# Wide products for expert_u up to tile 62, one piece of memory for both halves of the tokens, and another split of the subtraction between DVE and POOL

## The chip, the cores and the metric

The kernel runs on one core of a Trainium2 chip. The metric is the device time of one execution in microseconds. The engines are PE (TensorE, matrix products), DVE (VectorE), ACT (ScalarE), POOL (GpSimd) and SP (SyncE, which issues most of the DMAs). Each works through its own list of instructions in order, and they meet by semaphores only.

## The reference, cut to what matters

Two transformer blocks follow each other on 256 tokens of width 1024, in float32. The change is in the last part of the second block, a layer with 16384 small experts. Each is one row of `expert_u` and one row of `expert_v`.

```
q = rmsnorm(x) @ w_query                       # 8 heads, two halves of 128
s = scores of each half against 128 sub_keys   # per head: 128 + 128 scores
i1, i2, gates = top 16 of the 16 x 16 best pairs, softmax over them
a = gelu(rmsnorm(x) @ expert_u.T)              # 256 tokens x 16384 experts
out = x + sum over the 8 * 16 chosen (gate * a) * expert_v row
```

The kernel computes the activations of all 16384 experts densely, multiplies them by a map of gates that is zero nearly everywhere, and multiplies the result by `expert_v`. That is done so for 192 of the 256 tokens; the other 64 fetch their rows of `expert_v` by indirect DMAs.

## The kernel before

**Halves.** PE multiplies in a format of less than full precision (`fp32r`). So each operand is split in a high part (a copy in that format, made by ACT, `act_high`) and a low part (the rest, a subtraction). Three of the four products of parts are computed: high by high, high by low, low by high. The subtraction is in place on the tile, and its 2048 columns are divided: DVE (`dve_low`) takes the first `share_of(...)`, POOL (`pool_low`) the others, and PE waits for both (`lo_v`, `lo_g`). The share is `EVEN` = 1152 for the first `ROOMY` = 45 tiles of `expert_u`, 1536 for the others of it, and 2048 for `expert_v`.

**Tiles.** `expert_u` comes in 64 tiles of 1 MB (128 x 2048), each with two groups of 128 experts and eight chunks of the width. The first 45 go through a ring of five places in SBUF, the others through a ring of three, since the gate maps and activations (`W`) grow over the other places. A tile of the ring is loaded when the tile that had its place has been used by PE.

**Wide and narrow products.** In tiles 0 to 46 (`WIDE` = 47) the high part of a chunk is multiplied by both halves of the tokens at once, 512 columns (L1277, for the last chunk L1280), which land beside each other in PSUM, and its low part by the high half, 256 columns (L1278). The low sums are then copied out of PSUM by ACT (L2797, into `LP`) and added to the high ones by DVE (`add_halves`, L2141, both in PSUM and LP). After that ACT applies GELU (L2802, L2810). From tile 47 on three products of 256 columns each add up in PSUM themselves (`pe_pass3`, L546 to L548), and ACT applies GELU directly.

**Gate maps.** In tiles 47 to 62 each tile also has three maps (`early_quads`), each of four tokens: one-hot rows by ACT (two pieces, L2757 and L2761), DVE (L2108, L2110) and POOL (L2881), which PE multiplies (L1260) into banks 0 to 3. DVE then weighs the activations with them (L2120, L2121, L2128).

**Routing.** In tiles 1 to 46 DVE also finds the chosen experts, a piece for each tile (`ROUTING`, `dve_route`), for tokens 0 to 127 in tiles 1 to 23 and for the others in 24 to 46. Eight tiles of "lists" (MAX8 and the like), one of "pairs" (eight sums L2235), five of "heads" (MAX8 again), one of "gates", six of "select" (comparison L2270, eight products L2274, reduction L2276, and the same again), one of "share". After tiles 22 and 45 PE transposes what "share" left.

**Order of DVE in an iteration i.** `add_halves(i-1)`, then `dve_low` of tile i+1, then the routing piece (from tile 47 on: one-hots, weighing, `dve_low`). ACT: high part of tile i+2, then for tile i the copy of the low sums, waiting for DVE's sum, GELU. POOL: subtractions alone until tile 47. PE takes tile n when both subtractions are done and GELU of tile n-2.

Of the kernel before, what the change touches and what calls it, by code (L numbers as in the profile page):

```python
# [27 lines left out]
LAST_MAPS = MAPS_AT + DENSE // 4 // MAPS  # L28
WIDE = 47
ROOMY = 45  # L30
EVEN = 1152
MOE_PLACES = (0, 1, 2, 3, 4, 5, 6, 9, 10, 11, 12, 13, 14, 15)
# [167 lines left out]
def buffers(nc):  # L200
# [26 lines left out]
    m.HT = (fr(m.HH[:, :, :]), fr(m.HL[:, :, :]))  # L227
    m.HX = fr(halves[:, :, :, :]).rearrange("p x k t -> p k x t")
    m.Y = twin("y", [P, 2, D])
# [107 lines left out]
    m.SC = DS[:, 4096:8192].rearrange("p (b j n) -> p b j n", b=2, j=16)  # L337
    m.LP = [BIG[:, 19456 + 512 * i:19968 + 512 * i].rearrange("p (n t) -> p n t", n=2) for i in range(2)]
    m.W = BIG[:, 0:128 * DENSE].rearrange("p (n t) -> p n t", n=128)
# [33 lines left out]
def weight_tiles(a, m):  # L373
# [74 lines left out]
    last_in = lambda x: max([k for k in range(len(slot)) if slot[k] == x] + high_in.get(x, []))  # L448
    order = sorted((0, 1, 2, 5, 6), key=last_in)
    slot += [order[i % 5] for i in range(ROOMY)]  # L450
# [659 lines left out]
def tensor_second(nc, m, s, t, before, after):  # L1110
# [153 lines left out]
    for i in range(64):  # L1264
        tile = f["expert_u"] + i
        hi, lo = pe_halves(pe, m, s, t, tile)
        bank = act_bank(i)
        if i < 2:
            pe.wait_ge(s.sc, 6 + 2 * i)
        else:  # L1270
            pe.wait_ge(s.act, i - 1)
        for j in range(2 if i < WIDE else 0):
            o = m.PS[:, bank + j, :].rearrange("p (x t) -> p x t", x=2)
            for k in range(8):
                at = 1024 * j + 128 * k
                if k < 7:
                    pe.matmul(o, hi[:, at:at + P], m.HX[:, k], start=(k == 0), stop=False, skip_group_check=True)  # L1277
                ins = pe.matmul(o[:, 0], lo[:, at:at + P], m.HT[0][:, k, :], start=False, stop=False, skip_group_check=True)  # L1278
                if k == 7:
                    ins = pe.matmul(o, hi[:, at:at + P], m.HX[:, k], start=False, stop=True, skip_group_check=True)  # L1280
        for j in range(2 if i >= WIDE else 0):
            for k in range(8):
                at = 1024 * j + 128 * k
                ins = pe_pass3(pe, m.PS[:, bank, 256 * j:256 * j + 256], [x[:, at:at + P] for x in (hi, lo)],
                               [x[:, k, :] for x in m.HT], k == 0, k == 7)
        ins.then_inc(s.used, 2)
        for what, b, _ in ROUTING.get(i, ()):
# [58 lines left out]
def act_bank(i):  # L1346

    return 4 + 2 * (i % 2) if i < WIDE else 6 + i % 2


def act_columns(m, i):

    x, bank = m.PS, act_bank(i)
    return x[:, bank:bank + 2, 0:256] if i < WIDE else x[:, bank, :].rearrange("p (n t) -> p n t", n=2)


# [536 lines left out]
def vector_second(nc, m, s, t, before, after, own):  # L1893
# [62 lines left out]
    def beat(i, beats=BEATS2):  # L1956
        for what, u in beats.get(i, ()):
# [3 lines left out]
            elif what == "peerturn":  # L1961
                dve_turn(nc, m, s, "peer", m.g_ffn2, m.HT[1], m.HT[0])
            elif what == "outaturn":
# [174 lines left out]
    def add_halves(i):  # L2138
        bank = act_bank(i)
        ve.wait_ge(s.part, 1 + i + 1)  # L2140
        ve.tensor_tensor(m.PS[:, bank:bank + 2, 0:256], m.PS[:, bank:bank + 2, 0:256], m.LP[i % 2], ALU.add).then_inc(s.added, 1)  # L2141

# [463 lines left out]
def scalar_second(nc, a, m, s, t, before, after, own):  # L2606
# [35 lines left out]
    def beat(i, beats=BEATS2):  # L2642
        for what, u in beats.get(i, ()):
# [35 lines left out]
            elif what == "outaturn":  # L2679
                act_turn(nc, m, s, "outa", m.gkp[:, 8:16], m.HT[0])  # L2680
                act_group(nc, m, s, o, "outa", m.ossb, 1)
            elif what == "ME":
                if u == 12:
                    act_know(nc, s, "cross")
                act_mem_exps(u)
            elif what == "MC":
                act_mem_copy(u)
            elif what == "peernorm":
                act_know(nc, s, "ffn2")
                for b in range(2):  # L2690
                    ins = ac.activation(m.Y[:, b, :], m.X[:, b, :], ACT.Copy, scale=rs[:, b:b + 1])
                ins.then_inc(s.peer_n, 1)
            elif what == "peerturn":
                act_turn(nc, m, s, "peer", m.g_ffn2, m.HT[0])

# [79 lines left out]
    for i in range(64):  # L2775
        if i < ROOMY:
            act_high(nc, m, s, t, first + i + 2)
        elif i > ROOMY:
            act_high(nc, m, s, t, first + i + 1)
# [16 lines left out]
        if i < WIDE:  # L2796
            ac.activation(m.LP[i % 2], m.PS[:, act_bank(i):act_bank(i) + 2, 256:512], ACT.Copy).then_inc(s.part, 1)  # L2797
            ac.wait_ge(s.added, i + 1)
# [421 lines left out]
```

## Time and profile before

| | |
|---|---|
| median of 3 runs | 1590.06 us (1589.67 to 1591.22) |
| profiled execution | 1590.42 us |
| its span, first to last instruction | 1589.1 us |
| PE busy | 1528.3 us (96%) |
| DVE, ACT, POOL busy | 957.0, 715.4, 536.6 us |
| granted clock of PE, mean | 0.997 |

The span is what the trace shows of the execution. A busy share is a mean over stages with different limits. What an engine waits for stands in brackets in the timeline and in the view of waits; an engine that is not waited for may be idle without cost.

### The profile page before, as it was taken

What the parts mean: (1) busy time and instruction counts of PE and PEld (TensorE: products, weight loads), DVE (VectorE), ACT (ScalarE), POOL (GpSimd) and SP (SyncE); (2) the same over time, 40 slices, a digit from 0 to 9 for tenths busy, and PEclk for the clock granted to TensorE, in tenths of its full rate; (3) what the DMA queues carried; (4) which work ended last, traced back from release to release, by engine and by line L of the source; (5) the groups of instructions that cost most, each with busy time, mean ns of one, the idle gap of its engine ahead of it and who ended that gap; (6) DMA issues with size and microseconds to landing.
All of it is one profiled execution on the core that took longest, in us unless ns stands there. A gap on an engine that the chain in (4) does not pass through costs nothing.

```text
span 1589.1 us, 22128 instructions
## 1 busy us (share of the span) xinstructions
PE 1528.3 (96%) x8741; PEld 1170.4 (74%) x8741; DVE 957.0 (60%) x1658; ACT 715.4 (45%) x1091; POOL 536.6 (34%) x322
## 2 busy tenths in 40 slices
PE   8999999999889888999999999999999999999998
PEld 6789754445344333888989888888899988888886
DVE  5876522111111111767553699899777869999896
ACT  6666411101001100656452656556588855555544
POOL 4212000000000000413121434434487866888880
PEclk9999999999999999999999999999999999999999
DMA  8457999999999999744443666666443479999994
GB/s 314 145 185 266 399 374 420 421 422 421 422 421 421 421 421 415 255 144 165 141 158 118 237 197 197 200 198 197 144 141 120 163 285 327 359 363 361 359 377 154
DMA packets 100749, 446.85 MB, mean 281 GB/s; under 512 B 11536, under 2 KB 20240, under 8 KB 59040
## 3 DMA queue, kind: packets, MB, share of 16 engines
q1 hardware_dynamic: 86976, 405.96, 68.0%
q0 software_dynamic: 11264, 33.60, 5.7%
q10 hardware_dynamic: 2400, 5.81, 0.9%
q8 instruction: 72, 1.18, 0.3%
q14 instruction: 37, 0.30, 0.1%
HBM read 436.31 MB, written 8.91 MB: 280 GB/s over the span
## 4 chain that ended last, share of the span: by engine, by line
PE 76%; DMA 16%; DVE 4%; ACT 2%; issue 1%; SPq 0%; ACTq 0%; DVEq 0%
PE ps L785 12%; PE ps L1324 10%; PE ps L1277 10%; DMA fix<-in_w_up 7%; PE ps L1316 7%; PE ps L546 7%; PE ps L548 6%; PE ps L547 6%; PE ps L1278 6%; DMA big<-in_w_up 5%; PE ps L1260 3%; DMA halves<-in_w_up 2%; PE ps L1280 1%; PE ps L807 1%; PE ps L852 1%
## 5 line engine op out<-in xcount | busy, mean ns | idle before, releaser
L2853 POOL TENSOR_TENSOR big_parts<-big,fix_parts 128x896 fp32r<-128x896 f32 (+1 forms) x23 | 47.3, 2056 | 551.7 <-ACT fix_parts L2327 551.7
L785 PE MATMUL ps<-big 128*64 128x512 f32 x792 | 212.7, 594 | 19.2 <-DMA big<-in_w_up 8.4
L2327 ACT ACTIVATE fix_parts<-fix 128x2048 fp32r<-128x2048 f32 x71 | 136.0, 1919 | 75.9 <-PE ps L1324 46.2
L785 PEld LDWEIGHTS ps<-big 128*64 128x64 f32 x792 | 71.0, 137 | 131.9 <-issue 130.3
L1277 PE MATMUL ps<-halves_parts,fix_parts 128*128 128x512 f32 x434 | 155.8, 398 | 0.0
L1378 DVE TENSOR_TENSOR fix_parts<-fix,fix_parts 128x1536 fp32r<-128x1536 f32 (+2 forms) x72 | 140.0, 1946 | 23.1 <-ACT fix_parts L2327 19.8
L785 PE MATMUL ps<-fix,big 128*64 128x512 f32 x488 | 133.4, 594 | 9.4 <-DMA fix<-in_w_up 6.6
L2853 POOL TENSOR_TENSOR fix_parts<-fix,fix_parts 128x512 fp32r<-128x512 f32 (+1 forms) x47 | 89.0, 1895 | 155.7 <-ACT fix_parts L2327 145.3
L1856 DVE TENSOR_TENSOR big<-big,ps 128x512 f32<-128x512 f32 x16 | 11.0, 688 | 215.3 <-PE ps L785 215.3
L1278 PE MATMUL ps<-halves_parts,fix_parts 128*128 128x256 f32 x464 | 120.7, 281 | 0.0
L548 PE MATMUL ps<-halves_parts,fix_parts 128*128 128x256 f32 x416 | 117.6, 283 | 0.0
L2905 POOL DMA_INDIRECT small<-actkeep,tig x64 | 109.2, 1706 | 19.5 <-issue 19.5
L2327 ACT ACTIVATE fix_parts<-big 128x2048 fp32r<-128x2048 f32 x41 | 78.5, 1915 | 41.0 <-PE ps L1324 28.5
L1879 DVE SCALAR_TENSOR_TENSOR big_parts<-ps,small,big_parts 128x512 fp32r<-128x512 f32 x32 | 22.6, 747 | 119.8 <-ACT big_parts L2599 119.8
L1277 PEld LDWEIGHTS ps<-halves_parts,fix_parts 128*128 128x128 f32 x434 | 81.7, 188 | 17.1 <-issue 0.2
L2874 POOL DMA_INDIRECT big<-in_expert_v,tig x48 | 81.7, 1702 | 34.5 <-issue 13.1
L1278 PEld LDWEIGHTS ps<-halves_parts,fix_parts 128*128 128x128 f32 x464 | 87.6, 189 | 5.3
L785 PEld LDWEIGHTS ps<-fix,big 128*64 128x64 f32 x488 | 45.2, 137 | 60.9 <-issue 60.9
L2599 ACT ACTIVATE big_parts<-ps,small 128x512 fp32r<-128x512 f32 x32 | 20.2, 683 | 145.7 <-PE ps L785 145.7
L1378 DVE TENSOR_TENSOR big_parts<-big,fix_parts 128x2048 fp32r<-128x2048 f32 (+2 forms) x41 | 80.2, 1957 | 8.6 <-ACT fix_parts L2327 6.6
L2563 ACT ACTIVATE big<-ps,small 128x256 f32<-128x256 f32 x32 | 13.4, 470 | 151.3 <-PE ps L807 151.3
L1277 PE MATMUL ps<-halves_parts,x_parts 128*128 128x512 f32 x224 | 80.4, 398 | 1.1 <-ACT big L2745 1.1
(450 smaller groups left out, 4205.5 us busy)
## 6 DMA issues: line engine op xcount, KB each, us to landing
fix<-in_expert_u SPq DMA_DIRECT2D x46, 1024.0 KB
fix<-in_expert_v SPq DMA_DIRECT2D x38, 1024.0 KB
big<-in_w_down SPq DMA_DIRECT2D x36, 1024.0 KB, 26.0
big<-in_w_up SPq DMA_DIRECT2D x32, 1024.0 KB, 26.4
big<-in_w_gate SPq DMA_DIRECT2D x31, 1024.0 KB, 23.3
big<-in_expert_v SPq DMA_DIRECT2D x26, 1024.0 KB
fix<-in_w_up SPq DMA_DIRECT2D x23, 1024.0 KB, 26.4
fix<-in_w_gate SPq DMA_DIRECT2D x21, 1024.0 KB, 26.6
```

The lines of the kernel that those rows point to most:

```text
L546: pe.matmul(o, l[0], r[0], start=first, stop=False)
L547: pe.matmul(o, l[0], r[1], start=False, stop=False)
L548: return pe.matmul(o, l[1], r[0], start=False, stop=last)
L785: ins = pe.matmul(m.PS[64 * i:64 * i + 64, bank, :], lhs(h * k_of // 2 + k, i), view(t.place[t.slot[x]])[:, k, c0:c0 + 512], start=(h + k ...
L1277: pe.matmul(o, hi[:, at:at + P], m.HX[:, k], start=(k == 0), stop=False, skip_group_check=True)
L1278: ins = pe.matmul(o[:, 0], lo[:, at:at + P], m.HT[0][:, k, :], start=False, stop=False, skip_group_check=True)
L1316: ins = pe.matmul(m.PS[:, 2 + half, :], both[:, j, 0:P], v[y][:, 1024 * j + 512 * half:1024 * j + 512 * half + 512], start=(i + j + y == 0 ...
L1324: ins = pe.matmul(m.PS[:, half, :], both[:, j, P + P * x:2 * P + P * x], v[y][:, 1024 * j + 512 * half:1024 * j + 512 * half + 512], start ...
L1378: nc.vector.tensor_tensor(m.fr(x[:, 0:end]), x[:, 0:end], m.fr(hi[:, 0:end]).bitcast(F32), ALU.subtract).then_inc(s.lo_v, 1)
L2327: nc.scalar.activation(m.fr(t.high[n]), t.place[slot], ACT.Copy).then_inc(s.hi, 1)
L2853: nc.gpsimd.tensor_tensor(m.fr(x[:, at:2048]), x[:, at:2048], m.fr(hi[:, at:2048]).bitcast(F32), ALU.subtract).then_inc(s.lo_g, 1)
L2905: po.indirect_dma_start(m.pk[:, k:k + 1], None, acts, bass.IndirectOffsetOnAxis(m.aix[:, k:k + 1], 0)).then_inc(s.picked[k // 4 % 4], 16)
```

## The change

Six things change. Tiles 47 to 62 get the wide products too (`WIDE` = 63), beside the gate maps, with the copy of the low sums in another place (`low_part`). Five places serve tiles 0 to 46 (`ROOMY` = 47), and the high part of tile 47 is made an iteration earlier. DVE subtracts 512 columns instead of 1152 in these tiles, and POOL the other 1536 (`EVEN`). Tiles 0 and 1 write banks 0 to 3, and tiles 0 to 3 wait for fewer of the eight copies of the scores. The two halves of the tokens lie chunk by chunk beside each other, so that the 512 columns are one piece of memory and not two of 256.

```diff
-WIDE = 47
-ROOMY = 45
-EVEN = 1152
+WIDE = 63
+ROOMY = 47
+EVEN = 512
...
-    m.HX = fr(halves[:, :, :, :]).rearrange("p x k t -> p k x t")
+    m.HX = fr(halves[:, :, :, :].rearrange("p x k t -> p (x k t)")).rearrange("p (k x t) -> p k x t", k=8, x=2)
+    m.HTX = (m.HX[:, :, 0], m.HX[:, :, 1])
...
-    order = sorted((0, 1, 2, 5, 6), key=last_in)
+    order = sorted(range(3), key=last_in) + [5, 6]
...
-        if i < 2:
-            pe.wait_ge(s.sc, 6 + 2 * i)
+        if i < 4:
+            pe.wait_ge(s.sc, 2 + 2 * i)
...
-                ins = pe.matmul(o[:, 0], lo[:, at:at + P], m.HT[0][:, k, :], start=False, stop=False, skip_group_check=True)
+                ins = pe.matmul(o[:, 0], lo[:, at:at + P], m.HTX[0][:, k, :], start=False, stop=False, skip_group_check=True)
...
-    return 4 + 2 * (i % 2) if i < WIDE else 6 + i % 2
+    return 2 * i if i < 2 else 4 + 2 * (i % 2) if i < WIDE else 6 + i % 2
...
+def low_part(m, i):
+
+    return m.LP[i % 2 + (2 if i >= MAPS_AT else 0)]
...
-        if i < ROOMY:
+        if i < MAPS_AT - 1:
             act_high(nc, m, s, t, first + i + 2)
-        elif i > ROOMY:
+        elif i >= MAPS_AT:
             act_high(nc, m, s, t, first + i + 1)
...
-            ac.activation(m.LP[i % 2], m.PS[:, act_bank(i):act_bank(i) + 2, 256:512], ACT.Copy).then_inc(s.part, 1)
+            ac.activation(low_part(m, i), m.PS[:, act_bank(i):act_bank(i) + 2, 256:512], ACT.Copy).then_inc(s.part, 1)
```

DVE in two tiles of "select", before. L2141 is the sum of the parts, L1378 the subtraction (`fix` and `big` are places of the ring, `x_parts` and `fix_parts` high parts), L2274 and L2276 routing.

```order
L2141 TENSOR_TENSOR ps<-ps,big 128x2x256
L1378 TENSOR_TENSOR big_parts_51<-big,x_parts_54 128x1152
L2274 TENSOR_TENSOR big<-big,y 128x256 x8
L2141 TENSOR_TENSOR ps<-ps,big 128x2x256
L1378 TENSOR_TENSOR big_parts_51<-big,fix_parts_53 128x1152
L2276 TENSOR_REDUCE y<-big 128x128
```

The same tiles of the change (lines are six further down), and nothing has moved but the size of the subtraction:

```order
L2147 TENSOR_TENSOR ps<-ps,big 128x2x256
L1384 TENSOR_TENSOR big_parts_51<-big,x_parts_54 128x512
L2280 TENSOR_TENSOR big<-big,y 128x256 x8
L2147 TENSOR_TENSOR ps<-ps,big 128x2x256
L1384 TENSOR_TENSOR big_parts_51<-big,fix_parts_53 128x512
L2282 TENSOR_REDUCE y<-big 128x128
```

POOL at the first four tiles of `expert_u`, where only its size changes likewise, before:

```order
L2853 TENSOR_TENSOR fix_parts_53<-fix,x_parts_54 128x896
L2853 TENSOR_TENSOR fix_parts_53<-fix,fix_parts_53 128x896 x2
L2853 TENSOR_TENSOR big_parts_51<-big,x_parts_54 128x896
```

and in the change, each with 640 columns more:

```order
L2859 TENSOR_TENSOR fix_parts_53<-fix,x_parts_54 128x1536
L2859 TENSOR_TENSOR fix_parts_53<-fix,fix_parts_53 128x1536 x2
L2859 TENSOR_TENSOR big_parts_51<-big,x_parts_54 128x1536
```

ACT from the high part of tile 46 to GELU of tile 47, before (L2327 makes a high part, L2797 copies low sums, L2757 and L2761 are one-hots, L2802 to L2810 GELU):

```order
L2797 ACTIVATE big<-ps 128x512
L2802 ACTIVATE y<-ps 128x128
L2810 ACTIVATE big<-ps 128x384
L2797 ACTIVATE big<-ps 128x512
L2802 ACTIVATE y<-ps 128x128
L2810 ACTIVATE big<-ps 128x384
L2327 ACTIVATE fix_parts_53<-fix 128x2048
L2797 ACTIVATE big<-ps 128x512
L2802 ACTIVATE y<-ps 128x128
L2810 ACTIVATE big<-ps 128x384
L2327 ACTIVATE x_parts_54<-fix 128x2048
```

and in the change: the high part of tile 47 stands ahead of the copy of tile 45 and no longer behind its GELU.

```order
L2803 ACTIVATE big<-ps 128x512
L2808 ACTIVATE y<-ps 128x128
L2816 ACTIVATE big<-ps 128x384
L2333 ACTIVATE fix_parts_53<-fix 128x2048
L2803 ACTIVATE big<-ps 128x512
L2808 ACTIVATE y<-ps 128x128
L2816 ACTIVATE big<-ps 128x384
L2803 ACTIVATE big<-ps 128x512
L2808 ACTIVATE y<-ps 128x128
L2816 ACTIVATE big<-ps 128x384
L2333 ACTIVATE x_parts_54<-fix 128x2048
```

In tile 47 and after, ACT also gets the copy of the low sums (L2803) between the one-hots and GELU:

```order
L2763 ACTIVATE y<-ii,tig 128x128 x2
L2767 ACTIVATE y<-y,tig 128x128 x2
L2803 ACTIVATE big<-ps 128x512
L2808 ACTIVATE y<-ps 128x128
L2813 ACTIVATE big<-ps 128x24
L2816 ACTIVATE big<-ps 128x2x180
```

DVE gets the sum L2147 ahead of its one-hots there.

## Rows read from the trace of the kernel before

**Rows 1.** The page: busy time of each engine, share of the span, instructions.

```profile
PE 1528.3 (96%) x8741; PEld 1170.4 (74%) x8741; DVE 957.0 (60%) x1658; ACT 715.4 (45%) x1091; POOL 536.6 (34%) x322
```

**Rows 2.** Windows: busy us of PE, PEld, DVE, ACT, POOL; clock, DMA share, GB/s.

```profile
880.37:1146.30 265.93, 265.92 (x1510) 230.91 (x1510) 232.47 (x568) 150.05 (x193) 104.21 (x47) 1.00 0.58 190
1146.30:1282.40 136.10, 135.12 (x1153) 135.07 (x1153) 108.60 (x201) 113.44 (x259) 110.39 (x89) 1.00 0.44 141
```

**Rows 3.** Waits of PE from 880 to 1300: total us, times, longest.

```profile
PE ps L1277 <- ACT big L2745: 1.1, 1, 1.1
PE ps L546 <- issue: 1.0, 1, 1.0
```

**Rows 4.** Timeline of ACT, tiles 41 and 42: start, us, instruction, idle before and releaser.

```profile
1117.87 0.60 ACT L2797 ACTIVATE big<-ps 128x512 f32<-128x512 f32 x1 [0.63 <-PE ps L1280]
1119.24 0.28 ACT L2802 ACTIVATE y<-ps 128x128 f32<-128x128 f32 x1 [0.77 <-DVE ps L2141]
...
1119.78 1.92 ACT L2327 ACTIVATE fix_parts<-big 128x2048 fp32r<-128x2048 f32 x1
1123.51 0.60 ACT L2797 ACTIVATE big<-ps 128x512 f32<-128x512 f32 x1 [1.81 <-PE ps L1280]
```

**Rows 5.** Timelines of DVE, POOL and ACT around tile 17.

```profile
979.40 4.69 DVE L2274 TENSOR_TENSOR big<-big,y 128x256 f32<-128x256 f32 x8
984.01 0.68 DVE L2141 TENSOR_TENSOR ps<-ps,big 128x512 f32<-128x512 f32 x1
...
980.99 2.15 POOL L2853 TENSOR_TENSOR big_parts<-big,fix_parts 128x896 fp32r<-128x896 f32 x1 [2.73 <-ACT fix_parts L2327]
...
982.18 0.60 ACT L2797 ACTIVATE big<-ps 128x512 f32<-128x512 f32 x1 [1.27 <-PE ps L1280]
984.73 0.28 ACT L2802 ACTIVATE y<-ps 128x128 f32<-128x128 f32 x1 [1.95 <-DVE ps L2141]
```

**Rows 6.** Timeline of POOL: one subtraction of 896 columns, one of 512.

```profile
987.27 2.12 POOL L2853 TENSOR_TENSOR fix_parts<-fix,fix_parts 128x896 fp32r<-128x896 f32 x1 [4.14 <-ACT fix_parts L2327]
...
1242.82 1.29 POOL L2853 TENSOR_TENSOR fix_parts<-fix,fix_parts 128x512 fp32r<-128x512 f32 x1
```

**Rows 7.** Groups of DVE from 880 to 1147: busy us, mean ns of one, idle before.

```profile
L2270 DVE TENSOR_TENSOR big<-ii,y 128x2048 f32<-128x2048 f32 x4 | 9.1, 2279 | 0.0
...
L2276 DVE TENSOR_REDUCE y<-big 128x128 f32<-128x2048 f32 x4 | 9.1, 2272 | 0.0
...
L1378 DVE TENSOR_TENSOR fix_parts<-fix,fix_parts 128x1536 fp32r<-128x1536 f32 x2 | 3.5, 1752 | 2.5 <-ACT fix_parts L2327 2.5
```

**Rows 8.** Timelines of DVE and POOL ahead of tile 0, and PE's first product.

```profile
876.97 1.36 DVE L1378 TENSOR_TENSOR fix_parts<-fix,x_parts 128x1152 fp32r<-128x1152 f32 x1 [4.05 <-ACT x_parts L2327]
...
877.01 3.25 POOL L2853 TENSOR_TENSOR fix_parts<-fix,x_parts 128x896 fp32r<-128x896 f32 x1 [25.26 <-ACT x_parts L2327]
...
880.36 0.47 PE L1277 MATMUL ps<-halves_parts,x_parts 128*128 128x512 f32 x1 [1.09 <-ACT big L2745]
```

**Rows 9.** Timelines of PE and POOL: tile 46, and tile 48 with its maps.

```profile
1140.48 0.47 PE L1277 MATMUL ps<-halves_parts,fix_parts 128*128 128x512 f32 x1
...
1145.90 0.40 PE L1280 MATMUL ps<-halves_parts,fix_parts 128*128 128x512 f32 x1
...
1155.84 0.36 PE L546 MATMUL ps<-halves_parts,x_parts 128*128 128x256 f32 x1
...
1161.68 1.95 PE L1260 MATMUL ps<-big 128*128 128x128 f32 x16
...
1164.28 0.36 PE L546 MATMUL ps<-halves_parts,fix_parts 128*128 128x256 f32 x1
...
1144.34 2.84 POOL L2853 TENSOR_TENSOR fix_parts<-fix,fix_parts 128x512 fp32r<-128x512 f32 x1 [9.86 <-ACT fix_parts L2327]
```

**Rows 10.** Timeline of ACT behind tile 58: GELU, and the last one-hots.

```profile
1246.21 0.28 ACT L2802 ACTIVATE y<-ps 128x128 f32<-128x128 f32 x1 [1.42 <-PE ps L548]
...
1252.34 0.88 ACT L2761 ACTIVATE y<-y,tig 128x128 f32<-128x128 f32 x2
```

More of the change, by code:

```diff
@@ L337, in buffers @@
     m.SC = DS[:, 4096:8192].rearrange("p (b j n) -> p b j n", b=2, j=16)
-    m.LP = [BIG[:, 19456 + 512 * i:19968 + 512 * i].rearrange("p (n t) -> p n t", n=2) for i in range(2)]
+    m.LP = [x.rearrange("p (n t) -> p n t", n=2) for x in (BIG[:, 19456:19968], BIG[:, 19968:20480], DS[:, 0:512], DS[:, 512:1024])]
     m.W = BIG[:, 0:128 * DENSE].rearrange("p (n t) -> p n t", n=128)
@@ L1284, in tensor_second @@
                 ins = pe_pass3(pe, m.PS[:, bank, 256 * j:256 * j + 256], [x[:, at:at + P] for x in (hi, lo)],
-                               [x[:, k, :] for x in m.HT], k == 0, k == 7)
+                               [x[:, k, :] for x in m.HTX], k == 0, k == 7)
         ins.then_inc(s.used, 2)
@@ L1961, in beat @@
             elif what == "peerturn":
-                dve_turn(nc, m, s, "peer", m.g_ffn2, m.HT[1], m.HT[0])
+                dve_turn(nc, m, s, "peer", m.g_ffn2, m.HTX[1], m.HTX[0])
             elif what == "outaturn":
@@ L2140, in add_halves @@
         ve.wait_ge(s.part, 1 + i + 1)
-        ve.tensor_tensor(m.PS[:, bank:bank + 2, 0:256], m.PS[:, bank:bank + 2, 0:256], m.LP[i % 2], ALU.add).then_inc(s.added, 1)
+        ve.tensor_tensor(m.PS[:, bank:bank + 2, 0:256], m.PS[:, bank:bank + 2, 0:256], low_part(m, i), ALU.add).then_inc(s.added, 1)
     dve_low(nc, m, s, t, first)
@@ L2693, in beat @@
             elif what == "peerturn":
-                act_turn(nc, m, s, "peer", m.g_ffn2, m.HT[0])
+                act_turn(nc, m, s, "peer", m.g_ffn2, m.HTX[0])
     def product(tile, at=None, beats=BEATS2):
```

## The prediction

> **What bounds the kernel now.** I read the page first: PE is busy for 1528.3 of 1589.1 us, DVE for 957.0 [rows 1]. The windows then divide what the change touches: tiles 0 to 46 of expert_u (880.37 to 1146.30, 47 tiles) and tiles 47 to 62 with the gate maps (to 1282.40). PE is busy for 265.92 of 265.93 us in the first and 135.12 of 136.10 in the second [rows 2]. The view of waits has only two for PE in this stretch: 1.1 us ahead of tile 0 and 1.0 us ahead of tile 47 [rows 3]. So a faster DVE, ACT or POOL gives back at most 2 us here, and a slower one costs as soon as its slack is used up. Hence the question is how much slack there is, and that is read in the timeline.
>
> In a wide tile PE needs 5.64 us (1117.87 to 1123.51, the copies that start 0.03 us behind a tile's end). A tile's results go: copy of the low sums by ACT, sum by DVE, GELU by ACT 1.37 us after the copy began, and at 1.91 us the next high part, 1.85 us long [rows 4]. That releases DVE's and POOL's subtractions for a later tile. PE takes tile n+2 only when GELU of tile n is done: so DVE's sum may begin up to about 5.64 - 0.60 - 0.04 - 0.60 = 4.4 us behind a tile's end, where it begins about 0.67 us behind it in a plain tile. In some it is later already: tile 17's copy begins at 982.18, its sum at 984.01, and GELU waited 1.95 us for DVE [rows 5] against 0.77 us in a plain tile [rows 4].
>
> **What each part costs.** (a) *EVEN 512*. DVE subtracts 512 columns instead of 1152, POOL 1536 instead of 896, in tiles 0 to 44; in 45 and 46 POOL takes 1536 instead of 512. POOL takes 1.29 us for 512 columns and 2.12 for 896 [rows 6], so 2.12 + 640 x 0.83/384 = 3.50 us for 1536. DVE takes 1.36 us for 1152 when it comes first [rows 8] and 1.75 for 1536 [rows 7], so 0.67 for 512.
>
> By mere busy time that fits: POOL 3.5 of 5.64 us, and DVE gains 0.67 us a tile. But the two hold each other up. In tile 17 DVE runs eight equal products L2274. They take 4.69 us, and POOL's 2.15 us from 980.99 lies on them [rows 5]. Without a hold they follow each other at 0.335 us (each 256 columns at the 2.28 us that 2048 take [rows 7], and a little over), 2.68 us in all: the hold is 2.0 us, POOL's whole operation. It goes both ways: at 877.01 POOL started 0.04 us behind DVE's 1.36 us and took 3.25 instead of 2.12 us [rows 8]. The reduction L2276 reads one operand only; its four average 2272 ns, and POOL's 2.12 us at 987.27 lies on one of them unstretched [rows 6, 7]. So subtractions, L2235, L2270 and L2274, with two operands in SBUF, wait for POOL to finish and POOL for them; MAX8, reductions and sums on PSUM don't.
>
> The Trainium skill states this rule ("SBUF — State Buffer", section "SBUF: two separate sides"): DVE with two SBUF inputs and GpSimd exclude each other for a whole instruction. The trace agrees. By busy time alone this part would add 0 to the sum, by the rule what is worked out next.
>
> What DVE needs in an iteration that holds one whole POOL operation: sum 0.60, own subtraction 0.60, the routing piece, and 3.5 of hold. The routing pieces of "select" are 2.20 (L2270), 2.68 (eight L2274), 2.20 (L2276) [rows 7, 5]. That is 6.9, 7.4 and 6.9 us against a period of 5.64. Now it is 0.60 + 1.28 + 2.68 + 2.1 = 6.7 in the worst, and one tile of a reduction without a hold (4.1) repairs it. With the change no select tile is under 5.64, and six follow each other: (6.9 + 7.4 + 6.9 - 3 x 5.64) x 2 = 8.6 us late, for each of the two routing blocks. The tiles ahead of them, "pairs" and "heads", are late as well.
>
> I carried this forward tile by tile on paper, with these durations and three rules: whoever asks first runs its whole operation alone; POOL asks 3.3 us after DVE's sum began; PE starts tile n+2 after GELU of tile n. As a test, the kernel before comes out with the sum of tile 17 at 1.5 us behind the tile's end, where the trace has 1.87 [rows 5] (the end is 982.14), and without a stall, as in the trace [rows 3]. With the change, the sum of tile 9 comes at 2.7 us, 10 2.9, 11 0.9, 12 3.4, 13 1.4, 14 3.9, 15 2.0, 16 5.3, 17 6.9, 18 4.1, 19 5.8, 20 7.1, 21 4.1. From 16 on this is past 4.4: PE waits ahead of tiles 18 to 22 for 0.8, 1.6, 0.3, 1.1 and 1.6 us, and after tile 22, where its transposes need DVE's "share", for 3.8. In the second block (tiles 39 to 45) the same, with about 1.1 at the share: 9.3 + 6.6 = 15.9 us. Moving a queueing overhead by 0.02 us per operation, POOL's time by 0.1 us, or the hold that overlaps by 0.13 us gives 9 to 19 us. I take **+16**.
>
> (b) *The start.* Banks 0 to 3 for tiles 0 and 1 let PE start when two score banks are copied, not six. But POOL's first subtraction ended at 880.26, just before PE's start at 880.36 [rows 8]. It becomes 0.6 of hold + 3.5 - 0.15 = 3.97 us instead of 3.25: **+0.7**. Tile 1's, released by the same kind of copy, grows alike.
>
> (c) *Tile 47.* Its high part moves from iteration 46 to 45, so POOL's subtraction, which ran until 1147.18 [rows 9] while PE waited [rows 3], is long done: the 1.0 us wait goes. What is late next is ACT: from the end of tile 46 it needs 1.37 + 0.54 + 1.81 + 4.5 (twelve one-hot halves) = 8.2 us until the third map can run, so the maps of 47 end 9.1 us behind it instead of 9.5: **-0.4**.
>
> (d) *Wide tiles with maps.* Now a tile takes 8.44 us: 5.84 of products (1155.84 to 1161.68) and 2.60 of maps. Wide, right behind a pause of the same kind, it was 1140.48 to 1145.90 + 0.24 = 5.66 [rows 9]: PE's period becomes 8.26. ACT adds copy and wait, 1.37 us, to 6.91 of GELU, high part and one-hots (1246.21 to 1252.34 + 0.78) [rows 10]: 8.28. The two are even; before, ACT had 1.42 us to spare. DVE, busy for 108.60 us in these 16 tiles [rows 2], 6.8 each, gets 0.6 more and stays under it. 15 x (8.44 - 8.28) = **-2.4**. From both sides: nothing if ACT's chain is 0.16 longer, +2 if it is 0.3 longer.
>
> (e) *Layout of the halves.* The 512 columns become one piece of memory. A pair of products takes 5.64/16 = 0.3525 us in the steady stage, 0.347 right after a pause, both with the two pieces [rows 4, 9]. Two pieces thus cost nothing in one of the modes. I take 0; the other bound is 0.0055 x 16 x 47 = -4.1.
>
> The sum: 16 + 0.7 - 0.4 - 2.4 = +13.9 us. The profiled execution took 1590.42 us with a span of 1589.1, 0.4 above the median of 1590.06; on the median the forecast is 1604.0.
>
> **Rivals.** *No stalls* (ends on the other side): the sums stay under 4.4 us, because a DVE operation slips in more often between POOL's, or POOL's 1536 columns take under about 2.9 us. With 768 columns for DVE and 2.95 us for POOL my paper gives 4 to 10 us, so this is the point where it is decided. Then 0.7 - 0.4 - 2.4 = -2.1: 1588.0. For it: 0 stalls now. Against: a hold of a whole operation, seen in L2274 and in POOL's first subtraction. *No stalls and a faster layout*: -6.2, 1583.9. *Stalls, and the layout gains*: 1604.0 less 2 to 4, about 1601; a stalled tile gives back nothing. *Stalls of a smaller size*: one block's share wait vanishes, about 8 us in all: 1596. *The maps' stage slows*: DVE's longer iterations catch ACT's copy, +0.3 a tile: 1604.0 + 7 = 1611.
>
> **Chances.** Stalls as worked out 0.47, with the layout's gain 0.15, smaller stalls 0.13, slower maps as well 0.08, no stalls 0.12, no stalls and a faster layout 0.05. A measurement of this kernel tells 0.2% (3.2 us) from no change. Slower is the first four, 0.82 (0.01 of smaller stalls to "same"); same 0.12; faster 0.06. The range 1595 to 1611 takes in the first four and leaves out the last two; these bounds are also those of the stalls, 7 and 20 us, with the other terms.
>
> **What the profile after would show.** DVE subtractions of 512 columns and POOL's of 1536 at about 3.5 us; eight L2274 (some lines further down) taking 6.2 us; DVE's sums up to 7 us behind a tile's end; PE waits of 7 to 10 us ahead of tiles 18 to 23 and of 5 to 8 us ahead of tiles 41 to 46, put down to DVE or ACT; tile 0 at about +0.7; the wait ahead of tile 47 gone; 8.3 us from maps to maps. If PE shows no wait between tiles 16 and 23, step (a) is wrong; if the pair of products takes 0.347 us in a plain tile, (e) is.

## The result, and the profile after

| | before | after |
|---|---|---|
| median of 4 runs | 1590.36 us (1589.67 to 1591.22) | 1600.28 us (1599.96 to 1601.94) |
| ratio, 95% interval | | 1.0067 (1.0054 to 1.0079) |
| span of the profiled execution | 1589.1 us | 1598.7 us |
| granted clock of PE, mean | 0.997 | 0.995 |

The kernel became 9.9 us slower. The page of the kernel after, busy time of each engine (before: [rows 1]):

```profile
PE 1528.9 (96%) x8485; PEld 1158.1 (72%) x8485; DVE 976.7 (61%) x1674; ACT 722.2 (45%) x1107; POOL 587.9 (37%) x322
```

PE does as much as before. Where it stands still is in the windows of the kernel after: tiles 0 to 46, tiles 47 to 62 with the maps, and the rest (columns as in [rows 2], with the bounds set at the same places):

```profile
881.72:1159.68 277.96, 269.39 (x1511) 232.33 (x1512) 246.68 (x570) 148.13 (x192) 172.32 (x52) 0.99 0.55 181
1159.68:1292.94 133.26, 132.58 (x897) 120.99 (x896) 113.19 (x210) 118.83 (x272) 91.72 (x84) 1.00 0.43 143
1292.94:1598.65 305.71, 298.46 (x1338) 246.18 (x1336) 268.36 (x292) 157.19 (x147) 218.40 (x128) 0.99 0.89 332
```

Against [rows 2] tiles 0 to 46 are 277.96 - 265.93 = 12.03 us longer and the maps' stage 136.10 - 133.26 = 2.84 us shorter. Ahead of them lie 1.35 us more (881.71 against 880.36). What follows the maps is 1.0 us shorter (305.71 against 1589.1 - 1282.4 = 306.7). Sum: 12.03 - 2.84 + 1.35 - 1.0 = 9.5, the 9.6 of the spans.

PE's waits in the kernel after, from 870 to 1310 (before, [rows 3], there were two of about 1 us):

```profile
PE ps L1294 <- DVE y L2290: 4.7, 2, 3.4
PE ps L1278 <- ACT big L2816: 2.6, 4, 1.0
PE ps L1278 <- issue: 2.0, 1, 2.0
PE ps L1278 <- DVE fix_parts L1384: 0.6, 1, 0.6
PE ps L1278 <- DVE big_parts L1384: 0.5, 1, 0.5
PE ps L1261 <- ACT big L2767: 0.3, 1, 0.3
PE ps L1261 <- ACT y L2767: 0.3, 1, 0.3
```

The first line is the wait for "share" (3.4 us after tile 22, 1.3 after tile 45). The "ACT big" waits are those for GELU, which itself waits for DVE's late sum; "issue" is the start of tile 0, and the last two are waits for one-hots ahead of the second and third map of tile 47. Read by tile, PE stands ahead of 18, 19, 22 and 41, 42, 45 for 1.0, 0.55, 0.3 and 1.0, 0.55, 0.3 us. With the shares that is 8.5 us. POOL's and DVE's subtractions, from 881 to 1150, grouped; for DVE shortest, median and longest in ns:

```profile
L2859 POOL TENSOR_TENSOR fix_parts<-fix,fix_parts 128x1536 fp32r<-128x1536 f32 x19 | 69.4, 3657 | 41.9 <-ACT fix_parts L2333 41.9
...
L1384 DVE TENSOR_TENSOR big_parts<-big,fix_parts x12: 674/1424/3405, 900.2 to 1136.2; 128x512 fp32r<-128x512 f32 x12
```

The same 512 columns take DVE from 0.67 to 3.4 us. The timelines of DVE and of POOL around tiles 17 to 19 show why:

```profile
977.47 5.60 DVE L2276 TENSOR_TENSOR big<-ii,y 128x2048 f32<-128x2048 f32 x1
982.99 0.69 DVE L2147 TENSOR_TENSOR ps<-ps,big 128x512 f32<-128x512 f32 x1
983.59 0.68 DVE L1384 TENSOR_TENSOR big_parts<-big,x_parts 128x512 fp32r<-128x512 f32 x1
984.19 2.76 DVE L2280 TENSOR_TENSOR big<-big,y 128x256 f32<-128x256 f32 x8
986.87 0.69 DVE L2147 TENSOR_TENSOR ps<-ps,big 128x512 f32<-128x512 f32 x1
987.47 3.40 DVE L1384 TENSOR_TENSOR big_parts<-big,fix_parts 128x512 fp32r<-128x512 f32 x1
990.80 2.27 DVE L2282 TENSOR_REDUCE y<-big 128x128 f32<-128x2048 f32 x1
...
973.48 3.51 POOL L2859 TENSOR_TENSOR fix_parts<-fix,fix_parts 128x1536 fp32r<-128x1536 f32 x1 [4.43 <-ACT fix_parts L2333]
977.20 3.71 POOL L2859 TENSOR_TENSOR big_parts<-big,x_parts 128x1536 fp32r<-128x1536 f32 x1 [0.21 <-ACT x_parts L2333]
986.25 4.08 POOL L2859 TENSOR_TENSOR big_parts<-big,fix_parts 128x1536 fp32r<-128x1536 f32 x1 [5.34 <-ACT fix_parts L2333]
990.29 3.97 POOL L2859 TENSOR_TENSOR fix_parts<-fix,fix_parts 128x1536 fp32r<-128x1536 f32 x1
```

The comparison that begins at 977.47 takes 5.60 us instead of 2.28: until POOL ends at 980.91 it does nothing. DVE's subtraction at 987.47 takes 3.40 instead of 0.68, until POOL ends at 990.33. Then POOL's next waits for it (3.97 instead of 3.50), and the reduction at 990.80 runs at full speed beside POOL. That is a hold by whole operations.

### The profile page after: what moved, and what is told of

The parts are those of the page before. It is cut to its first block, busy times and chain, and to the rows that moved or that the text cites. A ratio compares the mean times of both kernels' runs of the same rounds, so it can differ in the third digit from the quotient of the medians.

```text
span 1598.7 us, 21648 instructions
## 1 busy us (share of the span) xinstructions
PE 1528.9 (96%) x8485; PEld 1158.1 (72%) x8485; DVE 976.7 (61%) x1674; ACT 722.2 (45%) x1107; POOL 587.9 (37%) x322
## 4 chain that ended last, share of the span: by engine, by line
PE 63%; DMA 16%; DVE 12%; POOL 4%; ACT 3%; issue 3%; SPq 0%; ACTq 0%; DVEq 0%
PE ps L786 12%; PE ps L1278 8%; PE ps L1325 7%; DMA fix<-in_w_up 7%; DMA big<-in_w_up 5%; PE ps L1317 5%; PE ps L547 5%; PE ps L1279 5%; PE ps L549 5%; PE ps L548 5%; PE ps L1261 3%; DVE fix_parts L1384 2%; POOL small L2911 2%; DMA halves<-in_w_up 2%; POOL big L2880 1%
## 5 line engine op out<-in xcount | busy, mean ns | idle before, releaser
L2859 POOL TENSOR_TENSOR big_parts<-big,fix_parts 128x1536 fp32r<-128x1536 f32 (+1 forms) x23 | 64.6, 2811 | 543.2 <-ACT fix_parts L2333 543.2
L1278 PE MATMUL ps<-halves_parts,fix_parts 128*128 128x512 f32 x588 | 212.6, 400 | 1.9 <-ACT big L2816 1.4
L1279 PE MATMUL ps<-halves_parts,fix_parts 128*128 128x256 f32 x720 | 187.0, 280 | 0.0
L2333 ACT ACTIVATE fix_parts<-fix 128x2048 fp32r<-128x2048 f32 x71 | 136.1, 1920 | 73.1 <-PE ps L1325 48.5
L2859 POOL TENSOR_TENSOR fix_parts<-fix,fix_parts 128x512 fp32r<-128x512 f32 (+1 forms) x47 | 113.7, 2420 | 126.9 <-ACT fix_parts L2333 116.7
L786 PE MATMUL ps<-fix,big 128*64 128x512 f32 x488 | 133.6, 594 | 9.2 <-DMA fix<-in_w_up 6.6
L1279 PEld LDWEIGHTS ps<-halves_parts,fix_parts 128*128 128x128 f32 x720 | 135.8, 189 | 7.1
L1278 PEld LDWEIGHTS ps<-halves_parts,fix_parts 128*128 128x128 f32 x588 | 111.1, 189 | 26.1 <-DVE fix_parts L1384 2.3
L1278 PE MATMUL ps<-halves_parts,x_parts 128*128 128x512 f32 x294 | 105.9, 399 | 4.0 <-issue 2.0
L1384 DVE TENSOR_TENSOR big_parts<-big,fix_parts 128x2048 fp32r<-128x2048 f32 (+2 forms) x41 | 85.2, 2080 | 9.5 <-ACT fix_parts L2333 8.7
L1325 PE MATMUL ps<-fix_parts,y_parts 128*128 128x512 f32 x268 | 78.4, 389 | 0.0
```

Source lines behind the costliest of these rows:

```text
L786: ins = pe.matmul(m.PS[64 * i:64 * i + 64, bank, :], lhs(h * k_of // 2 + k, i), view(t.place[t.slot[x]])[:, k, c0:c0 + 512], start=(h + k ...
L1279: ins = pe.matmul(o[:, 0], lo[:, at:at + P], m.HTX[0][:, k, :], start=False, stop=False, skip_group_check=True)
L1325: ins = pe.matmul(m.PS[:, half, :], both[:, j, P + P * x:2 * P + P * x], v[y][:, 1024 * j + 512 * half:1024 * j + 512 * half + 512], start ...
L1384: nc.vector.tensor_tensor(m.fr(x[:, 0:end]), x[:, 0:end], m.fr(hi[:, 0:end]).bitcast(F32), ALU.subtract).then_inc(s.lo_v, 1)
L2333: nc.scalar.activation(m.fr(t.high[n]), t.place[slot], ACT.Copy).then_inc(s.hi, 1)
L2859: nc.gpsimd.tensor_tensor(m.fr(x[:, at:2048]), x[:, at:2048], m.fr(hi[:, at:2048]).bitcast(F32), ALU.subtract).then_inc(s.lo_g, 1)
```

## The experiments

All are against the kernel before, run on the same chip. The stages in this table are worked out from each profiled execution: from the first product of tile 0 to the last of tile 46, to the end of the last map, to the end of the span. Their bounds differ from those of the windows above by up to 0.3 us.

| kernel | tiles 0-46 | 47-62 | rest | median us | ratio (95%) |
|---|---|---|---|---|---|
| before | 265.8 | 136.5 | 306.5 | | 1 |
| after | 277.8 | 133.6 | 305.5 | 1600.28 | 1.0067 (1.0054 to 1.0079) |
| e1 after, EVEN 1152 | 265.9 | 133.7 | 305.2 | 1587.77 | 0.9982 (0.9973 to 0.9991) |
| e2 before, EVEN 512 | 276.1 | 136.4 | 305.5 | 1600.87 | 1.0064 (1.0050 to 1.0077) |
| e3 e1, old layout | 265.7 | 133.7 | 306.1 | 1587.17 | 0.9980 (0.9971 to 0.9989) |
| e4 512 in calm tiles only | 265.9 | 133.7 | 305.8 | 1587.77 | 0.9985 (0.9976 to 0.9994) |
| e5 after, EVEN 768 | 272.6 | 133.6 | 305.4 | 1594.75 | 1.0036 (1.0023 to 1.0049) |
| e6 after, EVEN 1024 | 265.8 | 133.6 | 305.3 | 1586.65 | 0.9982 (0.9973 to 0.9991) |
| e7 POOL in two pieces | 273.2 | 133.6 | 305.1 | 1594.11 | 1.0036 (1.0023 to 1.0049) |
| e8 share's transposes later | 277.2 | 133.7 | 305.3 | 1598.73 | 1.0058 (1.0045 to 1.0071) |
| e9 the kernel after again | 278.8 | 133.7 | 306.7 | 1599.28 | 1.0061 (1.0047 to 1.0074) |
| e10 e1, tile 0 mostly on DVE | 266.6 | 133.6 | 305.1 | 1586.61 | 0.9982 (0.9972 to 0.9991) |
| e13 e1, WIDE 47 | 265.8 | 136.2 | 307.8 | 1588.68 | 0.9992 (0.9983 to 1.0001) |
| e14 e1, POOL works longer | 281.1 | 133.7 | 306.4 | 1603.30 | 1.0081 (1.0068 to 1.0095) |

The median of before was 1590.17 beside e1 to e4, 1589.16 beside e5 and e7 to e9, and 1589.87 beside the others; the ratios allow for it. Theory H is the prediction's: POOL's operation holds DVE's. The rest of the span varied from 305.1 to 307.8 with no pattern, so nothing is read from it.

**e1: the split alone undone.**

```diff
-EVEN = 512
+EVEN = 1152
```

> The changed kernel with EVEN back at 1152, all else as changed. Theory H (POOL's subtraction of 1536 columns holds DVE's operations with two operands in SBUF, so DVE's sums come late beside the routing pieces and PE waits): no wait of PE between tiles 16 and 23 or 39 and 46, tiles 0 to 46 in about 266 us as before, 8.25 us per tile with maps; 1590.4 - 2.9 (maps) - 0.4 (tile 47) = about 1587, the ratio to before 0.998. Rival R (the split is not what costs; the banks, the moved high parts, the slots or wide tiles with maps are): stays at about 1600.

Measured: 1587.77, ratio 0.9982. In the waits of PE all but the start and those ahead of the second and third map of tile 47 are gone:

```profile
PE ps L1278 <- issue: 1.0, 1, 1.0
PE ps L1261 <- ACT big L2767: 0.3, 1, 0.3
PE ps L1261 <- ACT y L2767: 0.3, 1, 0.3
```

The whole loss comes of the split, and without it the change would have been a gain of 0.2%.

**e2: the split alone made, in the kernel before.**

```diff
-EVEN = 1152
+EVEN = 512
```

> The kernel before with EVEN 512 and nothing else changed. Theory H: the same waits as in the changed kernel, ahead of tiles 18, 19, 22 and at both shares, about 8.6 us of waits, with the slower clock behind the first share and the start 12 to 13 us in all; 1602 to 1604. Rival R: within 1 us of the kernel before.

Measured: 1600.87, and PE's waits are those of the kernel after at the first share and ahead of 18, 19, 22, 41 and 42:

```profile
PE ps L1293 <- DVE y L2284: 3.4, 1, 3.4
PE ps L1277 <- ACT big L2810: 2.3, 3, 1.0
```

Theory H holds; its size was 1 to 3 us too high. The stage is 10.3 us longer and not 12, for the second share finds nothing to wait for. Here tiles 45 and 46 are still split 1536 to 512, so POOL's last two operations are short; that this is the reason is argued and not tested by itself.

**e3: the old layout under EVEN 1152.**

```diff
-    m.HX = fr(halves[:, :, :, :].rearrange("p x k t -> p (x k t)")).rearrange("p (k x t) -> p k x t", k=8, x=2)
-    m.HTX = (m.HX[:, :, 0], m.HX[:, :, 1])
+    m.HX = fr(halves[:, :, :, :]).rearrange("p x k t -> p x k t")
+    m.HTX = m.HT
```

> The changed kernel with EVEN 1152 and the halves in their old layout (the 512 columns of a product in two pieces again). The prediction's step (e), layout costs nothing: within 0.5 us of the same kernel with the new layout, 5.64 us per plain tile in both. Rival (one piece is faster, hidden in the changed kernel by stalls): 2 to 4 us slower than with the new layout.

Measured: 1587.17 against 1587.77, and 265.7 against 265.9 us for tiles 0 to 46. The layout gives nothing.

**e4: 512 columns where DVE has short pieces, 1152 elsewhere.**

```diff
-    return EVEN if 0 <= i < ROOMY else SHARE if i < 64 else 2048
+    busy = 8 <= i <= 24 or 31 <= i < ROOMY
+    return (1152 if busy else EVEN) if 0 <= i < ROOMY else SHARE if i < 64 else 2048
```

> The changed kernel with 512 columns for DVE only in tiles 0 to 7 and 25 to 30 of expert_u, whose subtractions stand beside the short lists, and 1152 in the tiles whose subtractions stand beside pairs, heads and select. Theory H: no wait of PE in tiles 16 to 46, the start 0.7 us later: about 1588. Rival (1536 columns on POOL cost in every tile, by contention with PE's or ACT's reads): 14 of 47 tiles keep 30% of the 12 us, about 1591.

Measured: 1587.77, stage 265.9, no wait of PE there. POOL's 3.5 us cost nothing in these 14 tiles, beside the lists. So the loss comes from the other 33, and the waits of PE above stand among those with long pieces that have two operands in SBUF.

**e5 and e6: other sizes.** EVEN 768 and 1024 in the kernel after.

> The changed kernel with EVEN 768: POOL subtracts 1280 columns, 2.12 + 384 x 0.83/384 = 2.95 us. Theory H: the same lateness, much smaller; the paper of the prediction gives 3 to 8.5 us of stalls, less what it over-counted with 512 (16 against 12): 1587.8 + 3 = about 1591. Rival T (a threshold that lies above 2.95 us): no wait, 1588. Rival in proportion to the columns moved: 0.6 of the 12.5 us, 1595.

> The changed kernel with EVEN 1024: POOL subtracts 1024 columns, 2.12 + 128 x 0.83/384 = 2.4 us. The rule carried forward on paper gives 0 to 1 us of stalls: 1588. Rival (the loss is in proportion to the columns moved, as 768 with 6.8 of 12 us might suggest): 0.2 x 12.5 = 2.5 us more, 1590.3.

Measured: 1594.75 with 768 and 1586.65 with 1024. The stage grows by 6.8 us with 768 and by nothing with 1024. So the loss is not in proportion to the columns: it begins between 2.39 us of POOL (1024 columns) and 2.95 us (768). With 768, H's number (1591) was too low, though the 6.8 us lie in the 4 to 10 that the prediction's paper gave, and the rival in proportion hit 1595 by chance, as 1024 then showed.

**e7: POOL's columns in two operations.**

```diff
-    nc.gpsimd.tensor_tensor(m.fr(x[:, at:2048]), x[:, at:2048], m.fr(hi[:, at:2048]).bitcast(F32),
-                            ALU.subtract).then_inc(s.lo_g, 1)
+    cuts = (at, (at + 2048) // 2, 2048) if at == EVEN else (at, 2048)
+    for lo, to in zip(cuts, cuts[1:]):
+        ins = nc.gpsimd.tensor_tensor(m.fr(x[:, lo:to]), x[:, lo:to], m.fr(hi[:, lo:to]).bitcast(F32), ALU.subtract)
+    ins.then_inc(s.lo_g, 1)
```

> The changed kernel with EVEN 512, POOL's 1536 columns subtracted in two operations of 768 (about 1.84 us each). Theory H (POOL holds DVE for a whole operation, and DVE can come in between two): DVE's compare is held 1.8 us instead of 3.5, its sum before it is not later; PE's waits fall to less than half: 1590 to 1595, although POOL is busy for 0.2 us longer per tile. Rival (both engines share the path by the amount of data, or POOL keeps it while it has work): 1600 or a little more.

Measured: 1594.11. POOL is busy for longer (191.8 us in tiles 0 to 46 against 172.3), and yet the stage is 4.6 us shorter. The same comparison as above, in the timeline of DVE of this kernel:

```profile
973.88 3.94 DVE L2276 TENSOR_TENSOR big<-ii,y 128x2048 f32<-128x2048 f32 x1
977.92 0.70 DVE L2147 TENSOR_TENSOR ps<-ps,big 128x512 f32<-128x512 f32 x1
978.53 1.54 DVE L1384 TENSOR_TENSOR big_parts<-big,x_parts 128x512 fp32r<-128x512 f32 x1
980.00 7.71 DVE L2280 TENSOR_TENSOR big<-big,y 128x256 f32<-128x256 f32 x8
```

It is held for one piece, 3.94 - 2.28 = 1.7 us instead of 3.3. The eight products, between which both pieces find a gap, take more instead (7.71 us); so six tenths of the loss stay, 7.4 of 12 us, where less than half was the claim for PE's waits. The time is in the range expected, 1590 to 1595.

**e8: the first share's transposes one tile later.** PE makes them behind tile 23.

```diff
-        for what, b, _ in ROUTING.get(i, ()):
+        for what, b, _ in ROUTING.get(i - 1, ()) if i == 23 else ROUTING.get(i, ()) if i != 22 else ():
             if what == "share":
```

> The changed kernel (EVEN 512) with TensorE's three transposes of the first share behind tile 23 instead of tile 22. The wait there was 3.4 us, and tile 23 then ran its first pairs of products at a granted clock of 0.5 (0.63 us a pair instead of 0.35). If both are paid only because PE stands still: the wait and the slow pairs go, 3.4 + 1.3 us, as DVE's sum of tile 22 begins 3.4 us behind the tile, under the 4.4 that are allowed: about 1595.5. Rival (the wait only moves: PE stands ahead of tile 23 or 24 for DVE's sum): 1599 to 1600.

Measured: 1598.73, stage 277.2. The 3.4 us wait went, but PE now waits 2.3 us ahead of tile 25, for ACT behind DVE:

```profile
PE ps L1278 <- ACT big L2816: 4.9, 5, 2.3
```

The rival held: the wait moved, to a tile later than it said, and the median lies 0.3 us under its range. DVE's "keys" and "sparse" pieces stand behind the transposes, so DVE waited with them; its sum of tile 23 then came 6.7 us behind the tile's end. I had looked at the sum of tile 22 and not at what is queued behind the moved wait.

**e9: the kernel after once more.** It was to have POOL's share cut to 896 columns; the edit did not get into the kernel, and what ran was the kernel after, unchanged.

> The changed kernel with EVEN 512, but POOL subtracts only columns 1152 to 2047 (columns 512 to 1151 get no low part subtracted: this part of the computation is left out). Tells the length of POOL's operation from what DVE does. Theory H: POOL holds DVE for 2.1 us, DVE itself works for 0.7 us less: no wait of PE, sums earlier than with EVEN 1152, about 1587.5. Rival (the lateness comes of the order in which DVE gets its work, not of POOL's length): 1600.

Measured: 1599.28, so it tells nothing of that expectation. It does tell how repeatable the lateness is. Its stage is 278.8 us against 277.8. At tile 9 POOL's subtraction starts 3.95 us behind the end of tile 8 in the one and 3.94 in the other, beside DVE's "pairs" sums, but it takes another time. The timeline of POOL in the kernel after, and then in this one:

```profile
936.76 4.67 POOL L2859 TENSOR_TENSOR fix_parts<-fix,fix_parts 128x1536 fp32r<-128x1536 f32 x1 [2.13 <-ACT fix_parts L2333]
```

```profile
934.95 3.64 POOL L2859 TENSOR_TENSOR fix_parts<-fix,fix_parts 128x1536 fp32r<-128x1536 f32 x1 [2.13 <-ACT fix_parts L2333]
```

In the one POOL waits 1.2 us for DVE's run of sums to end, in the other it gets in between two of them. The sum of tile 9 begins 0.7 us behind the tile's end in the one, as in a plain tile, and 2.8 in the other. Tiles 10 to 16 carry other numbers; from 17 on the sums of the first block are alike within 0.1 us. Of the 1.0 us by which the stages differ, this accounts for some 0.5 ahead of tile 23. Tile 23 itself gives 1.0 more, for PE ran at the lower clock for longer there, and the second block 0.5 less.

**e10: tile 0 mostly on DVE.** EVEN 1152, and in tile 0 alone 1920 columns on DVE.

```diff
-    return EVEN if 0 <= i < ROOMY else SHARE if i < 64 else 2048
+    return 1920 if i == 0 else EVEN if 0 <= i < ROOMY else SHARE if i < 64 else 2048
```

> The changed kernel with EVEN 1152, and in tile 0 alone 1920 columns on DVE. PE waited 1.0 us ahead of tile 0 there, for POOL's first subtraction, which took 1.2 us longer because DVE's stood before it. With 1920 columns (about 2.1 us) and then 128 on POOL (0.5 us) the pair ends about 0.7 us earlier: 0.7 us under the 1587.8 of EVEN 1152. Rival (another wait, the copies of the score banks, is as late): no gain.

Measured: 1586.61. In the timelines of DVE, POOL and PE tile 0 begins 2.6 us behind DVE's start, instead of 3.4 with 1152 [rows 8]:

```profile
876.44 2.16 DVE L1384 TENSOR_TENSOR fix_parts<-fix,x_parts 128x1920 fp32r<-128x1920 f32 x1 [3.84 <-ACT x_parts L2333]
876.49 2.43 POOL L2859 TENSOR_TENSOR fix_parts<-fix,x_parts 128x128 fp32r<-128x128 f32 x1 [25.06 <-ACT x_parts L2333]
...
879.01 0.47 PE L1278 MATMUL ps<-halves_parts,x_parts 128*128 128x512 f32 x1
```

But the stage is 0.7 us longer (266.6): PE then waits 0.75 us ahead of tile 1. The gain at the start is given back there, and the median alone (1.2 us under that of e1, which was run in another set, with intervals that overlap) can't tell it from nothing.

**e13: tiles with maps narrow again, with EVEN 1152.**

```diff
-WIDE = 63
+WIDE = 47
```

> The changed kernel with EVEN 1152 and WIDE 47, so that tiles 47 to 62 beside the maps have their sums made by three products each again. Tells the price of step (d). By the traces a tile with maps takes 8.43 us instead of 8.25: 15 x 0.18 = 2.7 us slower than the kernel with EVEN 1152 and wide tiles, 1590.4. Rival (the copy and sum of wide tiles are paid elsewhere, in the stage behind): no difference.

Measured: the stage takes 136.2 us instead of 133.6. The medians, 1588.68 here and 1587.77 of e1 in another set of runs, lie 0.9 apart with ratios of 0.9992 (0.9983 to 1.0001) and 0.9982; they agree with 2.6 us within their intervals and don't prove it. The trace does.

**e14: POOL longer, DVE's part as before.** EVEN 1152; POOL does a second operation, which multiplies 640 of its own columns with themselves, so that their low parts are no longer those of the reference.

```diff
...
+    if at == EVEN:
+        ins.then_inc(s.eps, 1)
+        nc.gpsimd.wait_ge(s.eps, n - t.split[t.first["expert_u"]] + 2)
+        ins = nc.gpsimd.tensor_tensor(m.fr(x[:, 1408:2048]), m.fr(x[:, 1408:2048]).bitcast(F32),
+                                      m.fr(x[:, 1408:2048]).bitcast(F32), ALU.mult)
+    ins.then_inc(s.lo_g, 1)
```

> The changed kernel with EVEN 1152, DVE's part as before, but POOL does a second operation on 640 of its columns, a product of the low part with itself (so the low parts of these columns are no longer those of the reference): 2.12 + 1.57 and a little between them, 3.8 us of POOL instead of 2.1. Tells POOL's hold from the size of DVE's own share. Theory H: stalls as with two pieces or worse, since DVE has 0.67 us more to do itself: 8 to 16 us, 1596 to 1604. Rival (POOL's length costs nothing; what costs is that DVE's part is short and its order changes): 1588 plus 1.7 for a later start, about 1590.

Measured: 1603.30, the stage 15.3 us longer than before. DVE had the same columns as in the kernel before, and PE waits for it:

```profile
PE ps L1278 <- DVE fix_parts L1384: 5.6, 5, 1.6
PE ps L1278 <- issue: 4.7, 5, 2.7
PE ps L1278 <- DVE big_parts L1384: 2.5, 2, 1.6
```

So POOL's longer work costs without any change of DVE's part. But DVE's part counts as well. In e7 POOL also had two operations, of 1.85 us each by the median against 2.13 and 1.26 here, and DVE 640 columns fewer; its loss was 7.4 us. Some 1.5 us of the 15.3 are of another kind: tile 0 took 7.4 us instead of 5.9, at a lower clock behind a wait of 2.7.

## Why the prediction was right, and which term was off

**(a) The hold: right in its mechanism, 4 us too large, and in its waits 7 us.** POOL's 1536 columns take 3.50 us (forecast 3.50), DVE's 512 take 0.67 when free (forecast 0.67, though the two rows named for it give 0.71). DVE falls behind in the select tiles of both blocks, and PE waits there for GELU, for DVE's subtraction and for the share. Measured 12.0 us where the step had 15.9: 7.5 in the first block (9.3) and 4.5 in the second (6.6). The mis-sized term is the carried lateness from tile 17 on. For tile 16 the paper had 5.3 us, and the trace has 5.1 (982.99; tile 16 ended at 977.93). For 17 it had 6.9, and the trace has 3.4 (986.87 against 983.50). The paper's two sums lie 5.64 + 1.6 = 7.2 us apart, with a whole hold among the eight products L2280. In the trace they are 3.9 apart: POOL's subtraction started at 986.25, with one product still to come, and was kept waiting until the eight were done (4.08 us instead of 3.50), so DVE took its sum first. The same happened at tile 40, and the eight products took 2.76 us in both. The 6.2 us foretold came in tiles 20 and 43 alone:

```profile
1000.86 6.08 DVE L2280 TENSOR_TENSOR big<-big,y 128x256 f32<-128x256 f32 x8
```

From tile 17 on the sums of the first block are 1.5 to 5.1 us less late than on the paper. PE waits 5.3 us from tile 18 to the first share, where the prediction named 7 to 10, and 3.1 from tile 41 to the second, where it named 5 to 8; the waits ahead of 20 and 21 (0.3 and 1.1) never came. So the rule of the paper that failed is "whoever asks first runs": beside a run of equal operations POOL asked first and came last.

Two terms that I didn't have work the other way. Of the 12.0 us only 8.5 are waits, against the 15.9 of the step, which was all waits; the other 3.5 hid nearly half of the error. For the larger part they lie behind the first share, where PE runs at a lower clock: tile 23 takes 10.94 us, of which 5.64 are products, 3.42 the wait and 0.33 the transposes, and 1.55 are left. Behind each shorter wait 0.2 us more go, and tiles 39 and 40 lose 0.3 each with hardly a wait (0.1 us or less).

The Trainium skill ("SBUF — State Buffer", section "SBUF: two separate sides") gives the rule of the lock, that the one who starts first has the ports for its whole instruction. e7 and e14 agree with it: one piece holds for 1.7 us, and more of POOL's work costs more though DVE's own is as before.

**(b) The start: right.** From POOL's start to PE's first product it is 881.71 - 877.67 = 4.04 us against 880.36 - 877.01 = 3.35 [rows 8], +0.7 as forecast. The other 0.66 of the 1.35 us lie ahead of the change; in e9, the same program, tile 0 began at 879.95.

**(c) and (d) Tile 47 and wide tiles with maps: right in sum.** A tile with maps takes 8.26 us, by the copies in ACT's timeline, where 8.28 was forecast:

```profile
1217.47 0.57 ACT L2803 ACTIVATE big<-ps 128x512 f32<-128x512 f32 x1
...
1225.73 0.57 ACT L2803 ACTIVATE big<-ps 128x512 f32<-128x512 f32 x1
```

The stage gave -2.84, forecast -2.8 (-0.4 and -2.4). The wait ahead of tile 47 is gone, with 0.7 us waited for ACT ahead of its second and third maps, as (c) said.

**(e) The layout: right.** 0 forecast, 0 measured (e3).

**The forecast.** 1604.0 was 3.7 us over the 1600.28, inside the range. That it came so near is in part luck: the waits were 7.4 us fewer than worked out, and 3.5 us that the sum did not have made up for nearly half of that. "No stalls", the rival on the other side, was what happens with the split undone: 1588.0 forecast, 1587.77 in e1 (the forecast had 0.7 us for a longer first subtraction, which e1 does not have). "Smaller stalls" (8 us, 1596) came about as near, by time, as the case that I called likeliest; its reason, a vanished share wait, is wrong for this kernel.

## What to carry to other kernels

Before an engine's work is moved to POOL, ask which operations of DVE with two operands in SBUF it will meet: its whole time counts as DVE's there, and what is saved on DVE (0.67 us a tile) can be less than what is lost to the hold (1.4 us more). Where both cannot be avoided, two shorter operations of POOL cost less than one (e7). Look at the busiest iteration, not the mean: with 2.39 us of POOL a tile nothing was lost, with 2.95 already 6.8 us. Of the kernels run, the changed one with EVEN 1024 (1586.65, ratio 0.9982) beats both, and so does that with 1152 (1587.77, the same ratio in its set of runs); they have the wide tiles' gain and none of the stalls.

## What the runs showed of the hardware that was not expected

**The one who asks first is not always the next.** POOL's operation slipped in between DVE's products in the kernel before (2.15 us, beside eight products of 4.69 us, [rows 5]) and did not in the kernel after (986.25, 4.08 us). At tile 17 that was no matter of chance. In the four kernels with all 1536 columns in one operation (after, e2, e8, e9) POOL started 0.04 to 0.06 us into the last product but one, at tile 17 and at tile 40, and was kept out all eight times (4.07 to 4.09 us). With three operations still to come it went both ways. In two executions of one program it did so at tile 9, and in one execution, the kernel after, at tiles 9 and 32, where POOL started 0.11 us into a sum both times: 4.67 us at 936.76, and here 3.65:

```profile
1074.26 3.65 POOL L2859 TENSOR_TENSOR big_parts<-big,fix_parts 128x1536 fp32r<-128x1536 f32 x1 [2.13 <-ACT fix_parts L2333]
```

What decides it is open.

**A standing PE can come back at the lower clock, and the length of the wait alone doesn't tell when.** Windows of the kernel after: the 3.4 us wait at the first share, the 2.7 us behind it, the rest of tile 23 (the column after POOL's is the clock):

```profile
1014.20:1017.60 3.40, 0.05 (x1) 0.00 (x0) 3.33 (x4) 0.60 (x1) 3.26 (x1) 0.96 0.68 214
1017.60:1020.30 2.70, 2.63 (x10) 2.34 (x11) 2.63 (x12) 2.05 (x3) 0.00 (x0) 0.50 0.37 143
1020.30:1025.00 4.70, 4.70 (x27) 4.12 (x27) 4.58 (x7) 0.41 (x1) 3.53 (x1) 0.95 0.00 0
```

For 2.7 us PE ran at 0.50 of its clock, 1.2 GHz, and a pair of products took 0.64 us instead of 0.35. In e8 the same followed a wait of 2.3 us; the windows there are the wait and the 3.1 us behind it:

```profile
1027.50:1029.90 2.40, 0.13 (x1) 0.00 (x0) 2.33 (x8) 0.76 (x3) 0.00 (x0) 0.99 0.01 3
1029.90:1033.00 3.10, 3.06 (x9) 2.69 (x10) 2.86 (x16) 2.18 (x2) 1.32 (x1) 0.50 0.64 156
```

But in e5 a longer wait, 2.57 us at the same share, was followed by full speed:

```profile
1012.50:1015.00 2.50, 0.00 (x0) 0.00 (x0) 2.49 (x2) 0.60 (x1) 2.36 (x1) 1.00 0.63 144
1015.00:1018.00 3.00, 2.94 (x19) 2.64 (x20) 2.93 (x12) 2.35 (x3) 0.00 (x0) 1.00 0.62 251
```

Waits up to 1.6 us were followed by full speed wherever I looked (e7, e14). In e9, the same program as the kernel after, the wait at the first share was 3.5 us, and the clock stayed at 0.50 for the next 3.9 us at least:

```profile
1017.00:1020.90 3.90, 3.90 (x14) 3.32 (x13) 3.76 (x14) 2.46 (x3) 1.33 (x1) 0.50 0.11 40
```

What decides between the two cases stays open. By these traces a wait of PE over 2 us cost up to 2.5 us on top (tile 23 of e9: 11.98 us from end to end, less 5.64 of products, 3.5 of wait and 0.33 of transposes).
